# Sixteen tokens taken out of a dense product and gathered instead, with thirty gathers issued ahead into idle buffers

## The reference, cut to what matters

```python
q = (ht @ w_q).reshape(t, 8, 2, 128)
sc = einsum('thid,hikd->thik', q, keys)              # 2 x 128 key scores for each token and head
top_s, top_i = top_k(sc, 16)
cand = top_s[:, :, 0, :, None] + top_s[:, :, 1, None, :]
best_s, best_pos = top_k(cand.reshape(t, 8, 256), 16)
i1 = take_along_axis(top_i[:, :, 0], best_pos // 16) # first key of the expert
i2 = take_along_axis(top_i[:, :, 1], best_pos % 16)  # second key
experts, gates = i1 * 128 + i2, softmax(best_s)
act = einsum('thkd,td->thk', u_tab[experts], h)      # a row of U for each of 128 picks of a token
coef = gates * gelu(act)
out = einsum('thk,thkd->td', coef, v_tab[experts])   # a row of V for each
```

## Time and profile before

| | |
|---|---|
| median of the runs shown | 2913.26 us |
| fastest run shown | 2910.97 us |
| the profiled execution, its own time | 2913.38 us |
| its span, first to last instruction | 2911.6 us |
| mean granted TensorE clock | 0.999 |
| PE, PEld, DVE, ACT, POOL busy | 99%, 92%, 86%, 50%, 34% |
| read from and written to HBM | 777.06 MB, 76.15 MB |

### The profile page before, as it was taken

The page is one execution under the profiler, slowest core; times in us unless marked ns, Lnnn a source line. Parts: engine busy times, 40 slices in busy tenths (PEclk is TensorE's granted clock), DMA queues, the critical chain, the costliest instruction groups (busy, mean ns, idle before and its releaser), DMA issues.

```text
span 2911.6 us, 49262 instructions
## 1 busy us (share of the span) xinstructions
PE 2870.6 (99%) x17930; PEld 2687.3 (92%) x17930; DVE 2498.5 (86%) x4769; ACT 1446.9 (50%) x2309; POOL 997.8 (34%) x774
## 2 busy tenths in 40 slices
PE   7999999999999999999999999999999999999998
PEld 4777789999999999999988788999999999999998
DVE  5667789799997899999987779988999879999998
ACT  3345234488884333333353532447888634333333
POOL 1000027644443334444400000675444433433442
PEclk9999999999999999999999999999999999999999
DMA  7434647899999999999932122679999999999996
GB/s 273 171 116 182 255 153 240 294 363 378 394 334 382 348 384 379 379 385 382 379 118 72 66 72 81 203 243 350 396 378 368 349 369 352 388 381 380 380 381 249
DMA packets 252524, 854.89 MB, mean 294 GB/s; under 512 B 25568, under 2 KB 58592, under 8 KB 245728
## 3 DMA queue, kind: packets, MB, share of 16 engines
q1 hardware_dynamic: 149280, 442.23, 41.5%
q0 software_dynamic: 98496, 381.73, 35.1%
q10 hardware_dynamic: 4608, 29.36, 2.4%
HBM read 777.06 MB, written 76.15 MB: 293 GB/s over the span
## 4 chain that ended last, share of the span: by engine, by line
PE 80%; DMA 9%; DVE 6%; ACT 3%; issue 2%; POOL 0%; SPq 0%; DVEq 0%; ACTq 0%
PE banks L1050 39%; PE banks L1582 27%; DMA w_raw<-wst 6%; PE banks L1550 4%; DMA ring<-u,gidx 2%; DVE w_lo L1623 2%; PE banks L1383 2%; PE banks L1120 1%; ACT w_hi L768 1%; PE banks L1066 1%; PE banks L1470 1%; DVE ring L2121 1%; DVE oneh L2143 1%; PE banks L1099 1%; DMA ada_buf<-adaw 1%
## 5 line engine op out<-in xcount | busy, mean ns | idle before, releaser
L768 ACT ACTIVATE w_hi<-w_raw 128x1024 fp32r<-128x1024 f32 x596 | 630.4, 1058 | 748.3 <-PE banks L1050 620.6
L1050 PE MATMUL banks<-hH,w_hi 128*128 128x352 f32 (+1 forms) x2528 | 867.7, 343 | 2.8 <-ACT w_hi L768 1.2
L1623 DVE TENSOR_TENSOR w_lo<-w_raw,w_hi 128x1024 fp32r<-128x1024 f32 x521 | 637.8, 1224 | 268.1 <-ACT w_hi L768 265.0
L1050 PE MATMUL banks<-hH,w_lo 128*128 128x352 f32 (+1 forms) x2528 | 846.7, 335 | 0.0
L1050 PE MATMUL banks<-hL,w_hi 128*128 128x352 f32 (+1 forms) x2528 | 846.5, 335 | 0.0
L721 POOL DMA_INDIRECT ring<-v,gidx x320 | 395.9, 1237 | 596.0 <-DVE vacc L2133 533.6
L721 POOL DMA_INDIRECT ring<-u,gidx x320 | 395.8, 1237 | 464.3 <-DVE gact L2121 448.2
L1050 PEld LDWEIGHTS banks<-hH,w_hi 128*128 128x128 f32 x2528 | 474.8, 188 | 50.1 <-issue 21.2
L1582 PE MATMUL banks<-c_lo_late,w_hi 128*128 128x352 f32 x1536 | 494.0, 322 | 0.0
L1050 PEld LDWEIGHTS banks<-hH,w_lo 128*128 128x128 f32 x2528 | 474.4, 188 | 19.6
L1050 PEld LDWEIGHTS banks<-hL,w_hi 128*128 128x128 f32 x2528 | 475.1, 188 | 17.3 <-issue 0.5
(11 more groups left out here) (347 smaller groups left out, 4025.8 us busy)
## 6 DMA issues: line engine op xcount, KB each, us to landing
w_raw<-wst SPq DMA_DIRECT2D x596, 512.0 KB, 6.4
...
```

Of the source, the lines that this page charges most:

```text
L768: nc.scalar.activation(w_hi[g % 2][:, :, :].rearrange("p a b -> p (a b)"), w_raw[:, g % RAWS, :], ACT.Copy).then_inc(s_wh, 1)
L1050: last = mm(bank[s][:, 0:t.stop - t.start], a[s][:, k, :], b[:, k, t], start=(k == 0 and a is w_hi and b is hH), stop=(k == KT - 1 and a i ...
L1623: v.tensor_tensor(w_lo[g % 2][:, :, :].rearrange("p a b -> p (a b)"), w_raw[:, g % RAWS, :], w_hi[g % 2][:, :, :].rearrange("p a b -> p (a ...
```

## The change

The last 16 tokens (`TAIL`) leave the dense U product, which is now 336 columns wide (`TU`); the V product keeps 352. Their 16 x 128 activations come from 16 more gathers of U in each layer (176 instead of 160). A gather places the picks of the 16 tokens on the 128 partitions, eight slots of 16; PE adds the sums back to a token's row through a matrix of slots, ACT takes Gelu, DVE multiplies the result into the gates before the one-hots are scaled, and the activation columns of the 16 tokens hold ones. New steps are `tail_rows`, `tail_operand` and `tail_sums` on PE, and `tail_gathers`, `tail_by_slot` and `tail_coefs` on DVE.

The first 30 gathers of a layer (`AHEAD`) go into 12 places in `stages`, which is idle until tile 42, and no longer into the ring; POOL issues 26 of them behind tiles 11 to 38 (16 before). DVE uses 6, 7 and 7 in rounds 1 to 3 (before 4, 5 and 5), 10 at tiles 37 to 41 (before 7), 105 in the gate stage (before 106) and 41 in the tail (before 33). `picked` works on two boxes, 8 x 8 and 8 x 16 places, 192 pairs for a head instead of 256. `unread` counts fall: 12 to 8 and 16 to 10 in the norms of layer 1 and at the end (12 to 8 alone), 6, 5, 19 to 5, 3, 13 at the start. At the start one `lo` moves from POOL to DVE.

```diff
+TAIL = 16
+TAIL_SLOTS = P // TAIL
+TU = TD - TAIL
-UG = HK + EXTRA
-GATHERS = 2 * UG
-EARLY_GATHERS = (0, 4, 5, 5)
+VG = HK + EXTRA
+UG = VG + TAIL
+GATHERS = UG + VG
+TAIL_AT = 32
+U_ORDER = [*range(TAIL_AT), *range(VG, UG), *range(TAIL_AT, VG)]
+EARLY_GATHERS = (0, 6, 7, 7)
+AHEAD = 30
+AHEAD_SLOTS = 12
-POOL_GATHER_AT = [12, 13, 14, 15, 16, 20, 21, 22, 23, 28, 29, 30, 31, 32, 36, 37]
+POOL_GATHER_AT = [11, 12, 13, 14, 15, 16, 17, 18, 19, 20, 21, 22, 23, 24, 25, 26, 27, 28, 29, 30, 31, 33, 34, 35, 37, 38]
-    U_GATHERS[_n] = 1 if _n % 2 else 2
+    U_GATHERS[_n] = 2
-    U_GATHERS[_n] = 2 if len(quads_of(_n + 1)) < 2 or _n % 4 == 2 else 1
+    U_GATHERS[_n] = 2 if len(quads_of(_n + 1)) < 2 or _n % 16 in (2, 6, 8, 12) else 1
-    U_GATHERS[_n] = 2 if _n % 5 in (1, 3) else 1
+    U_GATHERS[_n] = 2 if _n % 8 in (1, 3, 5, 6) or _n == GATE1 + 12 else 1
+TAIL_ROWS = GATE0 - 2
+TAIL_SUM = 60
+TAIL_MM = 90
+TAIL_COEF = 94
...
+        def gather_slot(l, k):
+            if k < AHEAD:
+                i = AHEAD_FROM + k % AHEAD_SLOTS
+                return stages[:, i // 8, :, :].rearrange("p e t -> p (e t)")[:, i % 8 * D:(i % 8 + 1) * D]
+            return ring[:, (l * (GATHERS - AHEAD) + k - AHEAD) % RING, :]
...
-            pool.wait_ge(s_wl, 1)
-            lo(0, 1)
             for c in range(KT, ADA_CHUNKS):
                 load_ada(0, c)
...
+                if AHEAD_SLOTS <= k < AHEAD:
+                    pool.wait_ge(s_gd, l * GATHERS + k - AHEAD_SLOTS + 1)
+                if k >= AHEAD + RING:
+                    pool.wait_ge(s_gd, l * GATHERS + k - RING + 1)
+                col = U_ORDER[k] if k < UG else k - UG
+                if k < UG and col == VG:
+                    pool.wait_ge(s_gidx3, l + 1)
...
-                    nc.scalar.activation(act_out[:, p % 2, n % 2, :], bank[n % 2][:, 0:TD], ACT.Gelu).then_inc(s_taken, 1)
+                    nc.scalar.activation(act_out[:, p % 2, n % 2, 0:TU], bank[n % 2][:, 0:TU], ACT.Gelu).then_inc(s_taken, 1)
...
-                    project(l, U0 + n, s, tokens=slice(TG, T))
+                    project(l, U0 + n, s, tokens=slice(TG, T - TAIL))
...
+                def tail_rows():
+                    pe.wait_ge(s_rt, l * (NT - 1) + NT - 1)
+                    mm(bank[3][:, 0:2 * HK], spread[:, :], route[:, 0:2, :].rearrange("p a j -> p (a j)"),
+                       start=True, stop=True).then_inc(s_xtr3, 1)
+                def tail_operand():
+                    pe.wait_ge(s_htv, l * 2 + 2)
+                    for k in range(KT):
+                        last = nc.tensor.transpose(bank[4 + k // 4][:, k % 4 * P:(k % 4 + 1) * P],
+                                                   tail_src[:, k * P:(k + 1) * P], ident[:, :])
+                    last.then_inc(s_htr3, 1)
+                def tail_sums():
+                    pe.wait_ge(s_tw, l + 1)
+                    mm(bank[4][:, 0:TAIL], tail_wide, tail_token_of[:, :], start=True, stop=True).then_inc(s_tt, 1)
...
                 scaled(0)
                 scaled(1)
+                if l == 0 and which == 0:
+                    lo(0, 1)
...
+                    boxes = [(slice(0, 8), 8), (slice(8, TOPK), TOPK)]
...
+                if n == TAIL_ROWS:
+                    tail_gathers()
+                if n == TAIL_SUM:
+                    tail_by_slot()
+                if n == TAIL_COEF:
+                    tail_coefs()
```

More of the change, by code:

```diff
@@ L222, in sem @@
             return ctx.enter_context(nc.semaphore(name))
+        banks = ctx.enter_context(nc.psum_tensor("banks", [P, 8, T], F32))
+        bank = [banks[:, i, :] for i in range(8)]
         ident = sb("ident", [P, P])
@@ L437, in build @@
         before_att.close()
-        banks = ctx.enter_context(nc.psum_tensor("banks", [P, 8, T], F32))
-        bank = [banks[:, i, :] for i in range(8)]
         s_const = sem("const_ready")
```

188 lines of the change are left out of this document (126 added, 62 removed).

## The result

The changed kernel takes 2922.43 us (median of five runs, 2916.8 to 2927.2) against 2910.97 for the kernel before beside it: 1.0038 times as long, 95% interval 1.0026 to 1.005. It is slower by 11 us where 20 us less were forecast, and 2.4 us above the range. The profiled execution is the fastest of the five, 2916.8 us with a span of 2915.1; it shows 3.5 us of the loss in its span.

A forecast was written before the change was run, and what follows sets the result against it. PE was taken as the bound, 80% of the chain. The terms -17 + 4 - 5 - 1.6 + 3.3 - 4.1 = -20.4 against 2913.4 gave 2893 us, range 2870 to 2920.

The forecast's parts named there:

- the gate stage's -17: Gate stage, 60 tiles a layer: narrower U tiles save 8.5 us a layer, 17 us for both.
- Rival A: Tail and gate stage: DMA engines become the bound, tail 106.5 us, gate stage gives back half; 2917 us in all, chance 0.23.
- the term (+4, measured +4.7): Tail, 26 tiles a layer: eight more gathers make it 98 us, +2 a layer, +4 us for both.
- B: Tail absorbs the added gathers as V's prefetch slips: tail 91.7 us, gate stage gains all; 2878 us in all, chance 0.17.
- C: Matmul spacing does not follow the columns, so 336 cost what 352 do; 2915 us in all, chance 0.08.
- Steps set at nothing: Four small DVE operations ahead of tile 42's `w_lo`, and `tail_coefs` before the first one-hots: ends 0 to +4, taken as nothing.
- the tail's own work on PE (3.3 by the prediction): PE's added transposes, float32 product and sums for the 16 tokens: 1.65 us a layer, +3.3 us.
- The clock: Clock at its upper level in all four windows; PE never rests long enough there for a change to be expected.
- Tiles 2 to 37: Tiles 2 to 38, bound by `w_lo` on POOL: a tile gains half, 0.08 us; -5 us over both layers.
- -1.65 for -1.1: Each norm of layer 1: fewer unread products let PE start earlier, -1.1 us.
- the 4.1 us that were forecast for norms, start and end: Fewer unread products in layer 1's norms and at the end, and `lo` on DVE at the start: -4.1 us together.

The follow-up runs named there:

- e10: The kernel before with U products 336 columns wide and nothing else changed; 2893.1 us, 0.9935 of the kernel before.
- e4: The changed kernel writing only an eighth of each stored matrix of gates in layer 1; 2911.9 us, 1.0001 of the kernel before.
- e9: The changed kernel with an eighth of a row in eight gathers of U fetched in tiles 102 to 117; 2908.2 us, 0.9993 of the kernel before.
- e5: The changed kernel with a semaphore for two places in `stages` instead of four; 2915.6 us, 1.0013 of the kernel before.
- e6: The changed kernel with activations stored and loaded 352 columns wide from tile 44 on; 2917.8 us, 1.0020 of the kernel before.
- e1: The changed kernel with its U products 352 columns wide again, ACT still reading 336; 2945.7 us, 1.0115 of the kernel before.
- e15: The changed kernel with two places to a semaphore and activations stored and loaded whole; 2911.9 us, 1.0000 of the kernel before.
- e8: The changed kernel with 19 instead of 13 unread products at one place at the start of layer 0; 2920.6 us, 1.0029 of the kernel before.

## Why the prediction was wrong

**The step that failed** is the gate stage's -17, with its sentence that DVE's "slack halves to 11 us but stays" and DMA's 376 GB/s are to be had because 389 were sustained elsewhere. It was 0. Two things were wrong in it. A column costs less: 4.9 ns for 16, so 7 us a layer and not 9.9 were there to gain. And the mean room on DVE and the DMA engines is not the room at a late transfer: with this stage's transfers a share of 0.97 went with 367 GB/s, so 376 would have asked for 0.99, and the 389 were those of 80 us of it. e10 and e4 show the size of each: the columns alone give 3 us a layer at a DMA share of 0.98, and all 7 (307.8 to 300.7) at 0.93. In layer 0 the loss can be counted: PE's waits of 5.2 us and one fall of the clock, 1.7, are the 7 us that the columns gave; in layer 1 the waits are 4.2 us, and the rest was not placed. The prediction read the 0.97 and put it into Rival A, but took PE's busy time for the bound because PE then never waited; a bound by two resources that are level looks so.

**Rival A** came nearest, 2917 for 2922, and its resource was the right one; its place was not. It put the loss into the tail at 382 GB/s. The tail moved 403, took 98.7 and 98.9 us, and the term (+4, measured +4.7) was right within a microsecond, its mechanism too (e9); there is luck in the last digit, as the kernel before had 95.0 us in one layer and 97.9 in the other. B and C fell: the tail did not absorb, and spacing followed the columns.

**Steps set at nothing.** The wait for four landings at once (`AHEAD_SET`) lies in the changed kernel's semaphores and was not priced: 6.8 us of median (e5). The split of a stored row into two packets was set at nothing: 4.6 us (e6), which is not clear of the noise, and e10, whose rows are stored whole, waits for stores as long. Whether the four operations of DVE at tile 40 cost anything was not told apart: PE waits 0.8 us at the first gate product of layer 0, and 1.4 in e10, which does not have them. Together with the tail's gathers (14 us, e9) these are 25.6 of the 29 us by which the changed kernel is longer than e10 (34 us at 352 columns, e1 against before). That such parts add up is seen for two of them alone (e15). In what is left the tail's own work on PE (3.3 by the prediction) and the table may lie; it was not split further.

**The clock** was dismissed with "PE never rests long enough". Behind the first 30 us PE now rests seven times for 1.8 to 3.2 us, and four times 1.7 us of clock go with it, so a wait of 2 us can cost nearly 4.

**What held, and what only came out.** Tiles 2 to 37 moved by -5.1 for -5, but not by half of a narrower tile, as was worked out: this came by luck. In layer 1 they take 139.3 us where they took 143.3, 0.11 us a tile, which is nearly all of the 24 x 4.9 ns = 0.118 us that a tile saves on PE, and in e10, with the columns alone, it is 3.8 and 4.1 us. Layer 1 before, after and in e10 (36 starts of Gelu):

```profile
L980 ACT ACTIVATE act_out<-banks x36: 443/446/469, 1827.0 to 1970.3; 128x352 f32<-128x352 f32 x36
L1020 ACT ACTIVATE act_out<-banks x36: 426/432/455, 1829.9 to 1969.3; 128x336 f32<-128x336 f32 x36
L980 ACT ACTIVATE act_out<-banks x36: 443/447/467, 1817.4 to 1956.5; 128x352 f32<-128x352 f32 x36
```

Layer 0 of the changed kernel gave 2.5 us back in two waits of PE for `w_lo`, which e5, e6, e8 and e9 (137.3 us and not 140.0) do not have:

```profile
497.23 0.39 PE L1094 MATMUL banks<-hH,w_hi 128*128 128x336 f32 x1 [1.44 <-POOL w_lo L756]
...
534.43 0.39 PE L1094 MATMUL banks<-hH,w_hi 128*128 128x336 f32 x1 [1.02 <-POOL w_lo L756]
```

Why a tile that waits for `w_lo` gains more than half was not found out. Norms: the first norm of layer 1, from its first product to the first projection, takes 7.45 us (1487.02 to 1494.47) where it took 9.10 (1482.73 to 1491.83, the end in the earlier trace rows); -1.65 for -1.1. At the start the small DVE operation takes 0.17 us, and PE's first product starts 1.3 us earlier, at 38.79:

```profile
35.03 0.17 DVE L1759 SCALAR_TENSOR_TENSOR gs<-mod,par 128x8 f32<-128x8 f32 x1
...
38.79 0.59 PE L1110 MATMUL banks<-hH,w_hi 128*128 128x512 f32 x1 [1.97 <-DVE hL L1719]
...
42.17 0.50 PE L1110 MATMUL banks<-hH,w_lo 128*128 128x512 f32 x1
```

Of the 4.1 us that were forecast for norms, start and end the whole kept 0.5: at the start the clock fell behind the idle time that fewer unread products left (eight matmuls at 0.43 us instead of 0.23), and V began with a wait of 1.2 us. The profile misses one thing: it is the fastest run, and the 5.6 us between it and the median were not seen in any trace.

The rule of the Trainium skill, "TensorE: Matmul & The Clock Gate", "Back-to-back issue gap", gave 2.1 ns for 16 columns as an estimate; the trace's 4.9 lies between that and the 6.9 worked out from rows 352 and 512 columns wide. The ceiling of 435 GB/s in the Trainium skill, "DMA: Bandwidth & Descriptors", "Specifications", agrees with the tail's 403; the limit of about 358 there does not.
